# Where ScalarE computes the exponential of an attention item: behind the copy of turned probabilities of its own place, or one place later

## The reference

```
for l in range(2):
    h = rms_norm(x); proj = h @ w_in + b_in          # 9292 columns
    A: 8 heads, softmax over the 128 keys that an indexer selects; o = p @ v
    B: 8 heads, s = q k^T / 8 + bias[h]; p = softmax(s); o = p @ v
    C: 4 heads, mLSTM (convolution and silu ahead of q and k, decay, no softmax)
    x = x + (sum_n sigmoid(gate_n) * (branch_n * silu(z_n)) @ w_branch_n) @ w_out
return rms_norm(x)
```

## Time and profile before

| | |
|---|---|
| median of 3 runs | 1283.41 us (1283.41 to 1283.66) |
| the profiled execution's own time | 1283.52 us |
| its span, first to last instruction | 1281.3 us |
| TensorE (PE) busy | 1263.1 us, 99% |
| VectorE (DVE) busy | 689.0 us, 54% |
| ScalarE (ACT) busy | 633.3 us, 49% |
| GpSimd (POOL) busy | 599.5 us, 47% |
| granted TensorE clock, mean | 0.999 |

### The profile page before, as it was taken

One profiled execution on the slowest core, in us unless ns is written; L12 is line 12 of the kernel. 1 busy time (PEld: TensorE's weight loads), 2 busy tenths in 40 slices (PEclk: granted clock), 3 DMA queues, 4 the chain that ended last, 5 costly groups with the idle time before them and its releaser, 6 DMA issues.

```text
span 1281.3 us, 19785 instructions
## 1 busy us (share of the span) xinstructions
PE 1263.1 (99%) x6486; PEld 1064.3 (83%) x6486; DVE 689.0 (54%) x1432; ACT 633.3 (49%) x1157; POOL 599.5 (47%) x759
## 2 busy tenths in 40 slices
PE   8999999999999999999999999999999999999997
PEld 6788888888988888888888888878888888888887
DVE  6799887745545221123687988785644631121144
ACT  6565676686534332333256466767754433323233
POOL 6654333423235555455775642333322455455463
PEclk9999999999999999999999999999999999999999
DMA  7223111221322323333342321122212222332331
GB/s 296 83 82 115 67 50 58 66 91 51 113 69 70 103 82 98 99 97 108 99 158 89 99 85 65 50 66 73 76 51 102 89 82 82 106 98 90 103 102 66
DMA packets 37047, 116.35 MB, mean 91 GB/s; under 512 B 4080, under 2 KB 4464, under 8 KB 36720
## 3 DMA queue, kind: packets, MB, share of 16 engines
q1 hardware_dynamic: 34672, 111.24, 26.3%
q10 hardware_dynamic: 2304, 4.20, 1.0%
HBM read 111.23 MB, written 4.19 MB: 90 GB/s over the span
## 4 chain that ended last, share of the span: by engine, by line
PE 92%; DVE 4%; ACT 2%; issue 1%; POOL 1%; DMA 0%; ACTq 0%; SPq 0%; DVEq 0%; POOLq 0%
PE acc L653 75%; PE ps_o L812 5%; PE ps_t L799 2%; PE ps_t L790 2%; PE ps_s L768 2%; PE ps_o L819 1%; PE ps_s L774 1%; DVE turn L1371 1%; DVE bk_lo_s L1351 1%; PE ps_s L757 1%; PE acc L686 1%; PE spare L750 1%; PE spare L831 1%; DVE prob L1392 0%; DMA xT<-x 0%
## 5 line engine op out<-in xcount | busy, mean ns | idle before, releaser
L604 POOL TENSOR_TENSOR w_lo<-w_raw,w_hi 128x256 fp32r<-128x256 f32 x744 | 586.0, 817 | 664.2 <-ACT w_hi L889 664.0
L653 PE MATMUL acc<-h_hi,w_hi 128*128 128x512 f32 x1120 | 447.6, 400 | 0.7 <-POOL h_lo L615 0.7
L653 PE MATMUL acc<-h_lo,w_hi 128*128 128x512 f32 x1120 | 438.8, 392 | 0.0
L653 PE MATMUL acc<-h_hi,w_lo 128*128 128x512 f32 x1120 | 292.6, 395 | 0.0
L889 ACT ACTIVATE w_hi<-w_raw 128x1024 fp32r<-128x1024 f32 (+1 forms) x210 | 202.0, 962 | 119.5 <-PE acc L653 90.8
L653 PEld LDWEIGHTS acc<-h_hi,w_hi 128*128 128x128 f32 x1120 | 210.7, 188 | 41.7 <-POOL h_lo L615 1.8
L653 PEld LDWEIGHTS acc<-h_lo,w_hi 128*128 128x128 f32 x1120 | 210.7, 188 | 39.4
L653 PEld LDWEIGHTS acc<-h_hi,w_lo 128*128 128x128 f32 x1120 | 205.6, 188 | 40.4
L1513 DVE SCALAR_TENSOR_TENSOR gated<-prob,acc 128x512 f32<-128x512 f32 x16 | 11.0, 688 | 246.7 <-PE acc L653 246.7
L1131 ACT ACTIVATE prob<-acc,par_half 128x512 f32<-128x512 f32 x48 | 33.1, 690 | 147.1 <-PE acc L653 147.1
L1078 ACT ACTIVATE prob<-prob,neg_max 128x128 f32<-128x128 f32 (+3 forms) x128 | 70.7, 553 | 9.2 <-DVE neg_max L1392 8.9
(11 more groups left out here) (274 smaller groups left out, 1823.0 us busy)
## 6 DMA issues: line engine op xcount, KB each, us to landing
w_raw<-w_full SPq DMA_DIRECT2D x162, 512.0 KB, 3.4
w_raw<-w_mix SPq DMA_DIRECT2D x48, 256.0 KB, 2.6
rel<-rel ACTq DMA_DIRECT2D x16, 256.0 KB, 2.9
xT<-x SPq DMA_DIRECT2D x4, 512.0 KB, 6.2
stage<-x_tok SPq DMA_DIRECT2D x4, 512.0 KB, 10.1
xT<-x SPq DMA_DIRECT2D x1, 2048.0 KB, 9.3
x_kept<-xT SPq DMA_DIRECT2D x1, 2048.0 KB, 9.0
xT<-x_kept SPq DMA_DIRECT2D x1, 2048.0 KB, 8.3
```

The lines of the kernel that those rows point to most:

```text
L604: last = pool.tensor_tensor(w_lo[:, slot, part, :], w_raw[:, raw, part, :], w_hi[:, slot, part, :].bitcast(F32), ALU.subtract)
L653: last = pe.matmul(acc[slot][:, :], w[:, slot, k, :], x[:, k, :], start=(place == 0), stop=(place == 3 * nk - 1))
```

## The change

Outside branch C the tuple of steps that a `push` adds is another. Before: the exponential of item n-1, then the turning (on ScalarE the copy) of item n-2, then the values of item n-3. After: the turning of item n-2, the values of item n-3, then the exponential of item n itself. All is written with `back` counted from the item just pushed, which is 1.

```diff
         mlstm = any(m is not None and m >= 64 for m in flying[-4:])
-        for back, kind in ((1, "exp"), (2, "turn_p"), (3, "values")) if mlstm else ((2, "exp"), (3, "turn_p"), (4, "values")):
+        for back, kind in ((1, "exp"), (2, "turn_p"), (3, "values")) if mlstm else ((3, "turn_p"), (4, "values"), (1, "exp")):
             if len(flying) >= back and flying[-back] is not None:
                 seq.append((kind, flying[-back]))
```

## The result

| | before | after |
|---|---|---|
| median (11 runs each, side by side) | 1283.41 us (1283.24 to 1284.76) | 1286.54 us (1286.24 to 1287.09) |
| ratio after / before, 95% interval | | 1.0024 (1.0016 to 1.0032) |
| profiled execution: its own time, its span | 1283.52, 1281.3 us | 1286.24, 1284.1 us |
| granted TensorE clock, mean | 0.999 | 0.997 |

The change costs 3.1 us; 2.9 were forecast. The sum is right, its terms are not: one was too small by 0.9 us in a layer, one was too large, and one that was put at nothing turned out a gain.

What follows compares the result with a forecast made beforehand. TensorE, busy 99% of the span, was taken as the bound. Per layer 0.36 + 0.7 + 0 + 0.4 = 1.46 us, two layers +2.9: 1283.5 + 2.9 = 1286.4 us, range 1283.0 to 1289.6.

Steps and rivals of the forecast that it cites:

- (a): Everywhere: a copy keeps the same work in front of it, so none comes earlier, whatever the exponential gains.
- (b): Every place: exponential waits for VectorE's maximum, with extras, unit's end and copy queued behind; costs where VectorE lags.
- the signs named: Line 799's waits gone; idle before line 1377 1.08 to 1.8; `neg_max` idle up; gaps at 26, 38, 41, 62; layers alike.
- Places 24 to 26: Per layer: item 24's maximum stays at 180.85, the copy of item 23 comes 0.67 later, the values +0.36 us.
- Places 35 to 41: Per layer: item 35's exponential delays the tanh, VectorE can't catch up, copies lag: +0.7 us, bounds -0.2 and +1.1.
- The copy moves by what the maximum moves: From item 39's maximum to item 38's copy ScalarE never idles, so the copy comes 0.7 to 1.0 us later.
- Places 47 to 50: Ten decay parts, 2.10 us, move behind item 47's exponential; its copy has the same sum ahead: 0.
- Places 57 to 62: Per layer: item 57's exponential waits for its maximum, item 56's copy comes about 2.0 later: +0.4 us, ends 0.3 and 1.3.
- The 1.3 us of the end: Item 59's exponential goes ahead of `y_split`, adding 1.3 us to the values at 302.01 if its maximum stays put.
- Rival 3: Moved `w_lo` pieces hold `y_split`'s low part at place 59 up to 1.06 us, or 1.3 us stays: slower, 15%.
- 1: Rival: the exponential was the tight step, so TensorE's waits for exponentials vanish: 1279.7 to 1280.3 us, 10%.
- 2: Rival: all is absorbed, no loss at 26 and 62, 35 to 41 replaces the old stall: 0 to +0.9 us, 25%.

Runs made afterwards that it cites:

- split held longer: Changed kernel, GpSimd's unit loop written out, unit 25's four `w_lo` pieces held until VectorE's product of place 23 is done: 1285.23 us.
- branch B alone: Kernel before, with only the exponentials of items 32 to 63 at their own place, those of items 0 to 31 one place later as before: 1284.03 us.
- the kernel with the exponential behind the taps: Changed kernel, with the exponential behind the extras only at the eight places per layer that hold a convolution's first tap: 1284.52 us.
- the split held: Changed kernel, GpSimd's unit loop written out, unit 25's pieces held until VectorE's pair of taps at place 22 is done: 1286.29 us; a second version has its own line.
- the control: Changed kernel with GpSimd's loop over units written out and nothing held: 1286.39 us.

## Why the prediction was right, and where it was not

**(a) Copies end the waits, so nothing is won.** Right. With exponentials early and of ScalarE's work only the unit's end behind them, the time is 1283.33 against 1283.34 us. The reason given, that a copy keeps the same work in front of it, was not exact: the work is the same, but the issue of `rel` cost ScalarE 0.38 to 0.43 us where it stood alone and nothing where it stands behind an exponential. The prediction counted it in both orders.

**(b) The extras queue behind a wait for the maximum.** Right, and with what follows from it, it is the whole loss: with the exponential behind the extras nothing is lost. Of the signs named, the waits of line 799 for exponentials are gone, ScalarE's idle time for `neg_max` is up from 8.9 to 73.0 us, and the values start 0.05 us behind a copy at places 26 and 38. At 41 they wait in layer 1 alone, at 62 in neither (the wait of that stretch stands at 59), and the layers are not quite alike.

**Places 24 to 26: forecast +0.36, measured +1.27.** The step that failed is "the maximum of item 24 ends at 180.85": I held VectorE fixed. It came 0.80 later, because the weight pieces of an earlier place moved over VectorE's taps. In the last part of the walk (57 to 62) I did follow the pieces, and here I did not.

Without that collision the loss by place 27 is 0.55 us (split held longer), and the rest closes. In that trace the copy of item 23 ends at 183.82 + 0.47 = 184.29 and the values start at 184.35; it is 0.39 ahead of the trace of before, so that is 0.46 later than before: the 0.36 of the walk and the 0.09 by which the maximum is still late. Another 0.10 comes behind the wait: six matmuls of values take 0.88 us in place of 0.78. The 0.22 us of places 23 and 24 (the same queue at the tap of place 21: the values of item 20 start 0.05 behind their copy), which the walk took for covered, don't come on top, since the copy sets the time at place 26.

That `w_lo` pieces stretch such an instruction of VectorE was already in the rows in another form (the pair at 1.84 us beside four pieces, 0.69 alone). The Trainium skill, page "SBUF — State Buffer", section "Who interferes with whom", has a VectorE instruction with two SBUF inputs contend with a GpSimd instruction that reads SBUF, by an exclusive lock. The direction holds here; the sizes measured are 0.69 to 1.11 us for one product and 1.54 to 2.25 for a pair, some 0.36 to 0.42 each, where a piece takes 2.81 / 4 = 0.70 to 3.27 / 4 = 0.82. Such an instruction thus loses about half a piece; what is locked, and for how long, no run here takes apart.

**Places 35 to 41: forecast +0.7, measured +0.46 and -0.11.** At place 38 the +0.7 came as worked out (+0.72 on the values of item 35 in layer 1). Two sizes were off, both by the issue: the idle time before the product grew by 0.33 in place of 0.7, and the copy of item 38 gained 0.43 us back, so that the wait at place 41, which layer 1 shows, is 0.43 us and replaces one of 0.78. "The copy moves by what the maximum moves" was the false step. That layer 0 keeps 0.46 and layer 1 nothing is the clock's doing, below.

**Places 47 to 50: forecast 0, measured -0.56 and -0.25 (from items 46 to 47).** The same error with the other sign on top: the issue of `rel` there is now under the exponential too. After, ScalarE at place 47:

```profile
257.37 0.73 ACT L1078 ACTIVATE prob<-prob,neg_max 128x512 f32<-128x512 f32 x1 [0.75 <-DVE neg_max L1392]
257.37 0.33 ACTq L1072 DMA_DIRECT2D rel<-rel  x1
...
258.57 2.10 ACT L1116 ACTIVATE decay_r<-decay 4x128 fp32r<-4x128 f32 x10
```

That saves 0.38 us ahead of the copy of item 47, behind which the values start in both layers. In layer 0 the rest is recovery: TensorE was late there from the slow clock, and by item 47 the copy sets the time again.

**Places 57 to 62: forecast +0.4, measured +0.45 and +0.36.** Right in size and mechanism: the copy of item 56 came 295.35 - 292.36 + 0.4 = 3.4 us later, of which 1.2 are the shift from earlier places, so 2.2 against the 2.0 forecast; the values lost 0.5. The 1.3 us of the end did not come. VectorE was faster once the pieces had left its pair: 0.45 us on the pair and 0.42 on the step behind it, 0.87 against the 0.9 estimated; that this is what saved the end is argued from the rows, no run tests it. Rival 3 is false: the low part of `y_split` took 0.69 us, untouched.

**Rivals.** 1 is false for this kernel, and half true elsewhere: with the `rel` issue last, exponentials do become the tight step and bring 0.8 us. 2 is false: places 23 to 27 alone lose 2.5 us over both layers, more than its upper end of 0.9. That the total was met is partly luck: an error of +0.9 in a layer at places 24 to 26 against errors that sum to -0.75 (layer 0) and -0.85 (layer 1) behind them.

**Left open.** Why layer 1 climbs by 0.26 us between items 38 and 46 (branch B alone and the kernel with the exponential behind the taps do it too), and why the values take 0.10 us more behind a wait.

## What to carry to other kernels

In a list that several in-order engines walk through, ask of every step that waits what is queued behind it: a wait moved one step forward costs whatever stood behind it, even if the step itself becomes earlier, and the waits listed for the bounding engine name only the last one to end. A DMA issue with a wait in it belongs behind the compute of its place (4.9 us here), and where it stands alone in the queue its own time counts. When work off the critical path moves, look for what it then lies beside: weight splits that slid by 1.1 us onto VectorE's taps made half the loss of branch A.

## What the runs showed of the hardware

**Behind a stall of TensorE the clock can fall, and the stall then costs more than its length for a while.** Windows of the kernel after, layer 0 (columns: stretch, its length, busy time and instructions of PE, PEld, DVE, ACT and POOL, granted clock, share of DMA, GB/s), and TensorE's first passes behind the wait of place 38:

```profile
223.00:226.00 3.00, 2.14 (x12) 1.58 (x10) 2.85 (x6) 2.83 (x6) 0.00 (x0) 1.00 0.02 6
227.60:230.40 2.80, 2.80 (x9) 2.23 (x9) 2.73 (x7) 1.87 (x6) 2.66 (x3) 0.50 0.00 0
231.50:234.50 3.00, 3.00 (x17) 2.50 (x17) 2.87 (x7) 1.89 (x5) 0.00 (x0) 1.00 0.55 186
...
228.24 0.63 PE L653 MATMUL acc<-h_lo,w_hi 128*128 128x512 f32 x1
228.66 0.63 PE L653 MATMUL acc<-h_hi,w_hi 128*128 128x512 f32 x1
```

After 1.55 us without a matmul the granted clock was 0.50, the 1.2 GHz level, for some 3.4 us: passes start 0.42 us apart in place of 0.23. In layer 1 of the same execution the same wait left the clock at 1.00:

```profile
856.98 0.77 PE L812 MATMUL ps_o<-bv,prob_t 128*128 128x64 f32 x5 [1.54 <-ACT prob_t L1102]
```

At item 36 layer 0 is 2.76 us late where layer 1 is 1.56, so the low clock costs 1.2 us at once; at item 38 a difference of 0.57 is left and at item 47 none, since TensorE waits less for copies in the layer that is later. In five further profiles with this wait (branch B alone, both with the split held, the control and the change with `rel` last) the clock fell in exactly one of the two layers; in the seven others, whose waits there are at most 1.14 us, it did not fall at these places. What decides between the layers no run here shows.

**An issue of a DMA from ScalarE's queue** takes 0.33 us and is free under the activation before it; with nothing before it, 0.38 to 0.43 us pass until the next instruction.
